# A hybrid diffusion block: attention by pairs of heads, with the mask added by the matrix engine and the results normalised in place of the probabilities

## What is computed

```
def sink_attention(q, ks, vs, masks, sink):
    scores = []
    for k, m in zip(ks, masks):
        s = jnp.einsum('bqgrd,bkgd->bgrqk', q, k).astype(F32)
        if m is not None:
            s = jnp.where(m, s, -jnp.inf)
        scores.append(s)
    sink_col = jnp.broadcast_to(sink...)
    p = jax.nn.softmax(jnp.concatenate(scores + [sink_col], axis=-1), axis=-1)
    ...  # out = sum over the key sets of p @ v
```

## Time and profile before

| | |
|---|---|
| median of three runs | 2300.29 us (2299.01 to 2300.86) |
| the profiled execution | 2299.07 us, its span 2297.3 us |
| TensorE busy | 2161.5 us, 94% of the span |
| VectorE busy | 1495.1 us, 65% |
| ScalarE busy | 1236.9 us, 54% |
| HBM read | 504.45 MB, 221 GB/s over the span |
| granted TensorE clock, mean | 0.964 |

### The profile page before, as it was taken

The page is one execution under the profiler, slowest core; times in us unless marked ns, Lnnn a source line. Parts: engine busy times, 40 slices in busy tenths (PEclk is TensorE's granted clock), DMA queues, the critical chain, the costliest instruction groups (busy, mean ns, idle before and its releaser), DMA issues.

```text
span 2297.3 us, 27395 instructions
## 1 busy us (share of the span) xinstructions
PE 2161.5 (94%) x11224; PEld 1729.8 (75%) x11224; DVE 1495.1 (65%) x1479; ACT 1236.9 (54%) x1394; POOL 45.7 (2%) x20
## 2 busy tenths in 40 slices
PE   6799999989899999988987999999999999999997
PEld 4678777767677777867566787887878787888875
DVE  3467777653332322245856887888878887888874
ACT  4566666642322222143545766676766666676763
POOL 0011111100000000000000000000000000000000
PEclk9899999979899999989997999999999999999998
DMA  8233454422244444325105999999999999999990
GB/s 301 94 129 129 148 185 173 173 94 74 87 170 165 166 169 155 107 74 175 48 1 193 345 344 356 330 364 334 342 340 342 339 338 350 336 362 333 344 344 21
DMA packets 137733, 509.61 MB, mean 222 GB/s; under 512 B 15296, under 2 KB 15680, under 8 KB 135296
## 3 DMA queue, kind: packets, MB, share of 16 engines
q1 hardware_dynamic: 137520, 507.65, 62.0%
q10 hardware_dynamic: 80, 0.13, 0.0%
HBM read 504.45 MB, written 3.28 MB: 221 GB/s over the span
## 4 chain that ended last, share of the span: by engine, by line
PE 83%; DVE 7%; ACT 4%; issue 1%; DVEq 0%; ACTq 0%
PE ps L1048 14%; PE ps L1046 14%; PE ps L1047 13%; PE ps L647 10%; PE ps L649 10%; PE ps L648 10%; DVE area L1742 3%; DVE d_lo L1613 2%; PE ps L957 1%; PE ps L975 1%; PE ps L1032 1%; PE ps L1105 1%; ACT area L1287 1%; PE ps L1075 1%; PE ps L659 1%
## 5 line engine op out<-in xcount | busy, mean ns | idle before, releaser
L2039 DVE TENSOR_TENSOR w_lo<-w_raw,w_hi 128x2048 fp32r<-128x2048 f32 x336 | 749.4, 2286 | 51.6 <-ACT w_hi L1496 50.7
L1496 ACT ACTIVATE w_hi<-w_raw 128x2048 fp32r<-128x2048 f32 x336 | 625.9, 1918 | 78.9 <-PE ps L1048 77.8
L1613 DVE TENSOR_TENSOR d_lo<-d_raw,d_hi 128x2048 fp32r<-128x2048 f32 (+1 forms) x76 | 171.9, 2262 | 334.4 <-ACT d_hi L1219 334.4
L1046 PE MATMUL ps<-w_hi,x_hi 128*128 128x512 f32 x896 | 357.1, 399 | 2.0 <-DVE x_lo L2095 2.0
L647 PE MATMUL ps<-h_top,d_hi 128*128 128x512 f32 (+1 forms) x816 | 331.5, 406 | 25.2 <-DVE h_low L1605 9.8
L1048 PE MATMUL ps<-w_hi,x_lo 128*128 128x512 f32 x896 | 355.0, 396 | 0.0
L1047 PE MATMUL ps<-w_lo,x_hi 128*128 128x512 f32 x896 | 350.7, 391 | 0.0
L1219 ACT ACTIVATE d_hi<-d_raw 128x2048 fp32r<-128x2048 f32 (+1 forms) x76 | 143.7, 1890 | 382.8 <-DMA d_raw<-in_dense 245.2
L649 PE MATMUL ps<-h_top,d_lo 128*128 128x512 f32 (+1 forms) x816 | 322.9, 396 | 0.0
L648 PE MATMUL ps<-h_low,d_hi 128*128 128x512 f32 (+1 forms) x816 | 319.1, 391 | 0.0
L647 PEld LDWEIGHTS ps<-h_top,d_hi 128*128 128x128 f32 x816 | 158.3, 194 | 69.6 <-issue 26.2
(11 more groups left out here) (266 smaller groups left out, 2571.9 us busy)
## 6 DMA issues: line engine op xcount, KB each, us to landing
w_raw<-in_experts SPq DMA_DIRECT2D x672, 512.0 KB, 5.7
d_raw<-in_dense SPq DMA_DIRECT2D x240, 512.0 KB, 5.3
area<-acum_rows SPq DMA_DIRECT2D x16, 1024.0 KB, 8.4
d_raw<-in_dense SPq DMA_DIRECT2D x8, 384.0 KB, 4.2
xT<-in_xt SPq DMA_DIRECT2D x4, 512.0 KB, 6.7
gate_rows<-area SPq DMA_DIRECT2D x4, 512.0 KB, 6.7
hT<-gate_rows SPq DMA_DIRECT2D x2, 1024.0 KB, 6.0
cst<-in_consts SPq DMA_DIRECT2D x2, 512.0 KB, 11.2
```

What stands on the lines that cost most here:

```text
L1046: mm(o, hi, w_hi[u % HIGH][:, a:a + 512], start=first, stop=False)
L1496: A(w_hi[n % HIGH][:], w_raw[n % RAW][:], ACT.Copy).then_inc(S["whi_done"], 1)
L1613: TT(d_lo[u][:, 0:w], d_raw[u][:, 0:w], d_hi[si % D_HIGH][:, 0:w].bitcast(F32), ALU.subtract)\
L2039: TT(w_lo[n % RAW][:], w_raw[n % RAW][:], w_hi[n % HIGH][:].bitcast(F32), ALU.subtract)\
```

## The change

A round is now a pair: both heads `a=0` and `a=1` of a query block, sixteen rounds `i` with `t, qt = i // 2, i % 2`.

- `scores(i)` issues the two score matmuls one behind the other, into two banks, and then adds the mask to the 128 columns that need it, by a matmul of an fp32r identity with the mask's block (`ident_r`, `band_r`). ScalarE makes those fp32r copies once, ahead of the loop.
- VectorE takes the maximum straight from PSUM (`maxima`), and ScalarE the exponential straight from PSUM, with the scale 1/8 in the instruction (`exp_pair`). The exponentials of the four sinks of a tile are one instruction.
- The probabilities are not scaled any more. `values(i)` runs over the key blocks, and in each over `a`. After two rounds, `denominators` makes four reciprocals, `spread_den` brings them by four matmuls over the 64 partitions of each head (columns 256 to 511 of the same bank), and `o_sum` copies the result to SBUF and multiplies it with them.
- The high and low parts are made from that (`o_high`, `o_lower`), one to two rounds later than the values.
- `sc` and `pT` have four tiles of 512 columns each, two to a round. `scores(i)` waits for the exponentials of round `i-2`, the transposes of a half for the copy of that half one round before.

```
-        sc = [a3.take(512) for _ in range(3)]
-        pT = [a3.take(512) for _ in range(2)]
-        stat = a3.take(24)
+        osum = [a3.take(256) for _ in range(2)]
+        stat = [a3.take(24) for _ in range(2)]
+        negs = a3.take(16)
+        keep_r = At(a3.n, 8192).n
+        ident_r = at("ident_r", place_of["area"] + 4 * keep_r, P, F32R)
+        band_r = at("band_r", place_of["area"] + 4 * (keep_r + P), 2 * P, F32R)
+        assert keep_r + 3 * P <= 8192
+        a3 = At(8192, 12288)
+        sc = [[a3.take(512) for _ in range(2)] for _ in range(2)]
+        pT = [[a3.take(512) for _ in range(2)] for _ in range(2)]
...
-            def turn(u):
-                pe.wait_ge(S["s_p"], u + 1)
-                if u >= 2:
-                    pe.wait_ge(S["s_ptc"], u - 1)
...
+            SC_BANK = ((0, 1), (6, 7))
...
+            def scores(i):
+                t, qt = i // 2, i % 2
+                if i >= 2:
+                    pe.wait_ge(S["s_exp"], 2 * i - 2)
+                for a in range(2):
+                    r = slice(64 * a, 64 * a + 64)
+                    mm(ps[SC_BANK[i % 2][a]][:], qT[r, t, qt * P:qt * P + P], kTt[r, t // 4, :], start=True, stop=False)
+                c = slice(256, 384) if qt else slice(384, 512)
+                for a in range(2):
+                    mm(ps[SC_BANK[i % 2][a]][:, c], ident_r[:], band_r[:, qt * P:qt * P + P], start=False, stop=True)\
+                        .then_inc(S["s_ps"], 1)
+            def turn(i):
+                for a in range(2):
+                    pe.wait_ge(S["s_exp"], 2 * i + a + 1)
+                    if i:
+                        pe.wait_ge(S["s_ptc"], 2 * i - 1 + a)
+                    for kt in range(4):
+                        last = pe.transpose(ps[2 + a][:, kt * P:kt * P + P], sc[i % 2][a][:, kt * P:kt * P + P], ident)
+                    last.then_inc(S["s_pt"], 1)
+            def values(i):
+                t, qt = i // 2, i % 2
+                pe.wait_ge(S["s_ptc"], 2 * i + 2)
+                if t >= 2 and qt == 0:
...
                 for kt in range(4):
...
+                    for a in range(2):
+                        kv = (t // 4) * 2 + a
+                        last = mm(ps[4 + t % 2][64 * a:64 * a + 64, qt * P:qt * P + P], vtk[:, kt, kv * 64:kv * 64 + 64],
+                                  pT[i % 2][a][:, kt * P:kt * P + P], start=kt == 0, stop=kt == 3)
                 last.then_inc(S["s_pv"], 1)
...
+            def spread_den(t):
+                pe.wait_ge(S["s_rd"], t + 1)
+                for qt in range(2):
+                    for a in range(2):
+                        c = 16 + 2 * qt + a
+                        last = mm(ps[4 + t % 2][64 * a:64 * a + 64, 256 + qt * P:256 + qt * P + P],
+                                  stat[t % 2][:, c:c + 1].to_broadcast([P, 64]), ident, start=True, stop=True)
+                last.then_inc(S["s_bc"], 1)
+            for i in range(18):
+                if i < 16:
+                    scores(i)
+                if 1 <= i < 17:
+                    turn(i - 1)
+                if i >= 2:
+                    values(i - 2)
+                    if i % 2:
+                        spread_den(i // 2 - 1)
...
+            act.wait_ge(S["band_in"], 32)
+            A(ident_r[:], ident, ACT.Copy)
+            A(band_r[:, 0:P], cst[:, C_BAND + 384:C_BAND + 512], ACT.Copy)
+            A(band_r[:, P:2 * P], cst[:, C_BAND + 768:C_BAND + 896], ACT.Copy).then_inc(S["mask_r"], 1)
...
+            def exp_pair(i):
+                t, qt = i // 2, i % 2
+                v = stat[t % 2]
+                for a in range(2):
+                    act.wait_ge(S["s_nm"], 2 * i + a + 1)
+                    if i >= 2:
+                        act.wait_ge(S["s_pt"], 2 * i - 3 + a)
+                    c = 2 * qt + a
+                    A(sc[i % 2][a], ps[((0, 1), (6, 7))[i % 2][a]][:], ACT.Exp, bias=v[:, c:c + 1], scale=0.125,
+                      accum_out=v[:, 8 + c:9 + c]).then_inc(S["s_exp"], 1)
+                if qt:
+                    act.wait_ge(S["s_sk"], t + 1)
+                    A(v[:, 12:16], v[:, 12:16], ACT.Exp).then_inc(S["s_ske"], 1)
+            def copy_pt(i):
+                for a in range(2):
+                    act.wait_ge(S["s_pt"], 2 * i + a + 1)
+                    if i >= 2:
+                        act.wait_ge(S["s_pv"], i - 1)
+                    A(pT[i % 2][a], ps[2 + a][:], ACT.Copy).then_inc(S["s_ptc"], 1)
...
-                act.wait_ge(S["s_pv"], 4 * t + 4)
-                A(o_top[:, t, :], ps[4 + t % 2][:, 0:256], ACT.Copy).then_inc(S["o_hi"], 1)
...
+                act.wait_ge(S["o_fp"], t + 1)
+                A(o_top[:, t, :], osum[t % 2], ACT.Copy).then_inc(S["o_hi"], 1)
+            for i in range(17):
+                if i < 16:
+                    exp_pair(i)
+                if i:
+                    copy_pt(i - 1)
+                if i % 2 and i >= 5:
+                    o_high(i // 2 - 2)
+            o_high(6)
             o_high(7)
...
+            TS(negs, sinkc, -1.0, None, ALU.mult).then_inc(S["negs_op"], 1)
+            dv.wait_ge(S["negs_op"], 1)
+            def maxima(i):
+                t, qt = i // 2, i % 2
+                v = stat[t % 2]
+                for a in range(2):
+                    u = 2 * i + a
+                    c = 2 * qt + a
+                    head = 8 * (t // 4) + 4 * a + t % 4
+                    dv.wait_ge(S["s_ps"], u + 1)
+                    dv.reduce_max(v[:, 4 + c:5 + c], ps[((0, 1), (6, 7))[i % 2][a]][:], AX.X).then_inc(S["s_mx"], 1)
+                    dv.wait_ge(S["s_mx"], u + 1)
+                    if t >= 2 and qt == 0 and a == 0:
+                        dv.wait_ge(S["s_bc"], t - 1)
+                    TS(v[:, c:c + 1], v[:, 4 + c:5 + c], -0.125, negs[:, head:head + 1], ALU.mult, ALU.min)\
+                        .then_inc(S["s_nm"], 1)
+                if qt:
+                    dv.wait_ge(S["s_nm"], 2 * i + 2)
+                    h0 = 8 * (t // 4) + t % 4
+                    sink2 = sinkc[:, h0:h0 + 5:4].unsqueeze(1).to_broadcast([P, 2, 2])
+                    TT(v[:, 12:16].rearrange("p (q a) -> p q a", q=2), v[:, 0:4].rearrange("p (q a) -> p q a", q=2), sink2,
+                       ALU.add).then_inc(S["s_sk"], 1)
+            def denominators(t):
+                v = stat[t % 2]
+                dv.wait_ge(S["s_ske"], t + 1)
+                TT(v[:, 8:12], v[:, 8:12], v[:, 12:16], ALU.add).then_inc(S["s_den"], 1)
+                dv.wait_ge(S["s_den"], t + 1)
+                dv.reciprocal(v[:, 16:20], v[:, 8:12]).then_inc(S["s_rd"], 1)
+            def o_sum(t):
+                dv.wait_ge(S["s_bc"], t + 1)
+                b = ps[4 + t % 2]
+                if t >= 2:
+                    dv.wait_ge(S["o_out"], t - 1)
+                    dv.wait_ge(S["o_hi"], t - 1)
+                dv.tensor_copy(osum[t % 2], b[:, 0:256]).then_inc(S["o_cp"], 1)
+                dv.wait_ge(S["o_cp"], t + 1)
+                TT(osum[t % 2], osum[t % 2], b[:, 256:512], ALU.mult).then_inc(S["o_fp"], 1)
...
             def o_lower(t):
                 dv.wait_ge(S["o_hi"], t + 1)
-                TT(o_low[:, t, :], ps[4 + t % 2][:, 0:256], o_top[:, t, :].bitcast(F32), ALU.subtract)\
+                dv.wait_ge(S["o_fp"], t + 1)
+                TT(o_low[:, t, :], osum[t % 2], o_top[:, t, :].bitcast(F32), ALU.subtract)\
                     .then_inc(S["o_out"], 1)
...
+            for i in range(16):
+                maxima(i)
+                if i % 2 == 0 and i:
+                    denominators(i // 2 - 1)
+                if i % 2 == 0 and i >= 4:
+                    o_sum(i // 2 - 2)
+                if i % 2 and i >= 5:
+                    o_lower(i // 2 - 2)
+            denominators(7)
+            o_sum(6)
+            o_lower(6)
+            o_sum(7)
             o_lower(7)
```

More of the change, by code:

```diff
@@ L947, in _ @@
             pe.wait_ge(S["v_out"], 4)
[L949 to L958, removed]
-            def turn(u):
-                pe.wait_ge(S["s_p"], u + 1)
-                if u >= 2:
-                    pe.wait_ge(S["s_ptc"], u - 1)
-                for kt in range(4):
-                    last = pe.transpose(ps[2 + u % 2][:, kt * P:kt * P + P], sc[u % 3][:, kt * P:kt * P + P], ident)
-                last.then_inc(S["s_pt"], 1)
@@ L968, in values @@
[L968 to L976, removed]
-                last.then_inc(S["s_pv"], 1)
@@ L979, in _ @@
[L979 to L985, removed]
+            SC_BANK = ((0, 1), (6, 7))
+            pe.wait_ge(S["mask_r"], 1)
+            def scores(i):
[9 more added lines that the diff above has]
+                        .then_inc(S["s_ps"], 1)
@@ L1457, in _ @@
             dense_high(W0 + 49)
[L1459 to L1468, removed]
@@ L1470, in o_high @@
-            def o_high(t):
-                act.wait_ge(S["s_pv"], 4 * t + 4)
-                A(o_top[:, t, :], ps[4 + t % 2][:, 0:256], ACT.Copy).then_inc(S["o_hi"], 1)
```

(39 more changed lines are left out.)

3 lines of the change are left out of this document (2 added, 1 removed).

## The result

The changed kernel takes 2268.99 us (median of four runs, 2268.68 to 2270.54), the kernel before 2300.12 us in the same comparison. The ratio is 0.9866 (95% interval 0.9854 to 0.9878), 31 us less. The profiled execution took 2270.54 us, its span is 2268.7 us; the one of before took 2299.07, so 28.5 us less there.

The account below looks back on a forecast made before the run. The prediction took TensorE to bound the attention loop: 16 x 3.55 + 6.4 + 2.5 = 65.7 us against 93.4, gain 27.7, so 2271.4 from the profiled 2299.07 us, 2272 against the median; range 2266 to 2284 (8 in 10).

Parts of the forecast that it names:

- Score pair: In the attention loop on TensorE, the two heads' score matmuls run side by side and take 1.05 us per pair.
- Values: In the attention loop on TensorE, sixteen alternating value records take what eight took, 1.01 us per pair.
- Transposes: In the attention loop on TensorE, eight transposes in one section take 1.05 us per pair.
- Spread: On TensorE, the four matmuls spreading the reciprocals cost 0.44 us per two pairs, 0.22 per pair.
- The sum: TensorE's work per pair in the loop, all parts added: 3.55 us against 5.40 before.
- Waits 2.5: TensorE waiting in a few rounds, 0.1 to 0.6 us each; 2.5 us put on the whole loop.
- nearly even: In a loop round, ScalarE's last copy done after 3.6 us (3.8 with sink exponential); TensorE needs it after 3.77.
- Start: At the loop's start the clock stays at half speed for 12.8 us, 6.4 us of lost work.
- Rival A: Softmax chain bounds the loop, PSUM reads being dearer; a round 4.2 to 4.3 us, 2284 us in all; chance 0.10.
- B: One of two TensorE overlaps fails, in the scores or in values and spread: 2284 to 2286 us; chance 0.09.
- C: Neither TensorE overlap happens, so the change only adds mask and spread: 2 us slower, 2301 us; chance 0.04.
- D: Slower: the clock is halved nearly throughout the loop, 114 us against 93.4, 2319 us in all; chance 0.06.

## Why the prediction was right

Forecast 2272, measured 2268.99; the forecast case is the one that came. By its steps:

- Score pair 1.05: measured 1.06. The overlap on rows, read from the first scores alone, was right. In the run with scores apart, losing it cost 24 us, the clock's share included.
- Values 1.01: measured 0.92 to 1.02, the lower with the spread behind. The row from the SSD stage carried over.
- Transposes 1.05: measured 1.00. The change of shape is paid by the mask, whose 0.28 stands against 0.22; its two matmuls start 0.16 apart, where 0.11 had been named as a sign.
- Spread 0.22 per pair: measured 0.27, since the value records ahead of it run into it and its first records pair late.
- The sum: 3.58 measured, 3.55 forecast.
- Waits 2.5: measured 1.8 in five places, which shows, twice in the middle of the loop, as 4.35 us from one score pair to the next where others take 3.81 (the prediction's signs had up to 4.0). The sum behind "nearly even" was a little off: its terms for the last copy add up to 3.64 us before any handover, so some 3.8 against 3.77, not 3.6. The two such rounds in the middle of the loop went when VectorE's result steps were moved, as the forecast had it.
- Start: this step was off. 6.4 us were put on the low clock, from 12.8 us of it. It lasted 6.0 us into the loop, so 3.0. That the clock rose early was luck: nothing in the prediction had it but the lower end of its range. TensorE had fewer gaps in its first rounds than before, but this is not shown to be the cause: with the scores apart it had none, and the clock stayed low for 19.7 us. 16 x 3.58 + 3.0 + 1.8 is 62.1, and 62.7 was measured, below the 64 to 68 that had been named as a sign of being right.
- In the profiled execution the later start (2.25 us) covered most of the difference, so 2271.4 came near 2270.5 for two reasons that cancel; against the medians the gain was 31.1 where 27.7 had been worked out.
- Behind the loop nothing moved: 66.63 us in both.

Rival A did not come: neither reader got dearer from PSUM. B and C were real alternatives, and three runs take the overlaps away: 2276 and 2293 for one lost (the first of them only half), 2307 for both, against 2284 to 2286 (by its own terms 2283 to 2287) and 2301 in the prediction. B undershoots for the scores because losing their overlap also brings two changes of shape a round, 5.3 us, and a longer low clock, 6.8. D did not come; the clock held at 1.00 from 1093.6 us to the end of the loop.

What stays open: why the first matmuls of most profiled executions start 1.7 us later than in the one of before, and what sets how long the clock stays low, at the start of the loop and behind it.

## What to carry to other kernels

Read from the trace whether two half-array matmuls already run side by side anywhere, and price a reordering by that place; the order of instructions is worth as much as their number (38 us between two orders of the same work here). A relief of the second engine gives next to nothing while the first one bounds, but it decides how few rounds the pipeline needs. Ahead of a loop on TensorE, look for work of another engine that could come later, and fill what idle time is left, if the clock falls in it.

## What was not expected of the hardware

- TensorE took a record of the free half from four places further down in the order, and here no further: with eight records of one half ahead of eight of the other, the second half began 0.49 us in, with the fifth record, and the section took 1.51 us against 1.02 in turn.
- A change of shape between two 64-row matmuls and back cost over a third of the matmul itself: 1.19 us for the second score matmul on its own, of which 0.86 are its records.
- With 3.0 us of idle time ahead of the scores the clock went to 0.50 and stayed there for the first 6.7 us of the loop; with three matmuls in that time it stayed at 1.00.
- After the same idle time of 7.1 us the clock stayed at 0.50 for the first 6.0 us of the loop with pairs, 12.8 before and 19.7 with the scores apart, where TensorE was busy 23.9 of the 24 us from 1087 on.
